# First stage: the output gate's modulation computed as rows, with waits for zeros and for a square root at other places

## The reference, cut to what matters

```
mod_lat = silu(c) @ mod_w + mod_b          # one row of 3072 for the tokens
mod_c   = silu(c_ctx) @ mod_w + mod_b      # one row of 3072 for the context
sh, sc, gt = split(mod, 3)                 # shift, scale, output gate (1024 each)
p = (layer_norm(x) * (1 + sc) + sh) @ w_in # 4224 columns: pooling, RWKV, HGRN, gate
y_rwkv, o_hgrn = the two recurrent branches, both directions, over context and tokens
mix = concat(pool, y_rwkv, o_hgrn) * silu(g)
x = layer_norm(ALPHA * x + gt_l * (mix @ w_out)) * ln_g + ln_b
```

## Time and profile before

| what | value |
|---|---|
| runs, median | 1694.6 us |
| profiled execution, its own time | 1697.69 us |
| its span | 1695.9 us |
| TensorE busy in the span | 1627.6 us (96%) |
| VectorE, ScalarE, GpSimd busy | 466.8, 325.7, 19.3 us |
| mean granted TensorE clock | 0.974 of full speed |
| DMA, share of 16 engines over the span | 33%, 191.29 MB |

### The profile page before, as it was taken

How to read it: one execution, slowest core, us unless ns; L and a number is a source line. 1 busy time by engine, 2 the same in 40 slices (tenths; PEclk the granted TensorE clock), 3 DMA queues, 4 the chain that set the end, 5 groups by cost and what they waited for, 6 DMA issues and landing times.

```text
span 1695.9 us, 26099 instructions
## 1 busy us (share of the span) xinstructions
PE 1627.6 (96%) x11627; PEld 1303.0 (77%) x11627; DVE 466.8 (28%) x1053; ACT 325.7 (19%) x689; POOL 19.3 (1%) x33
## 2 busy tenths in 40 slices
PE   7999998889799899999999999999999999999998
PEld 2544587778689687777788888888778778888887
DVE  2431023565652414124232000001402423200001
ACT  1201222443432311033300000001104330000000
POOL 2000001000000000000000000000000000000000
PEclk9999969989899999999999999999999999999999
DMA  9221330000002533433243444453343324344440
GB/s 332 103 89 60 107 117 2 3 2 3 17 25 80 126 114 135 149 113 136 100 149 128 157 155 156 149 127 123 126 149 121 128 100 149 136 157 154 149 162 25
DMA packets 110879, 191.29 MB, mean 113 GB/s; under 512 B 20888, under 2 KB 27296, under 8 KB 110640
## 3 DMA queue, kind: packets, MB, share of 16 engines
q1 hardware_dynamic: 109776, 188.29, 32.1%
q0 software_dynamic: 960, 1.33, 0.2%
q10 hardware_dynamic: 32, 0.01, 0.0%
HBM read 188.57 MB, written 1.05 MB: 112 GB/s over the span
## 4 chain that ended last, share of the span: by engine, by line
PE 79%; issue 16%; DVE 2%; ACT 1%; POOL 1%; DVEq 1%; POOLq 0%; ACTq 0%
PE psum L1071 28%; PE psum L1215 13%; PE psum L1156 9%; PE psum L793 5%; PE psum L1079 4%; PE psum L718 3%; PE psum L1239 2%; PE psum L954 1%; PE psum L1142 1%; PE psum L1185 1%; PE psum L709 1%; PE psum L1098 1%; PE psum L974 1%; ACT arena L1704 1%; PE psum L877 1%
## 5 line engine op out<-in xcount | busy, mean ns | idle before, releaser
L1071 PE MATMUL psum<-arena 128*128 128x256 f32 x2208 | 480.6, 379 | 0.0
L1071 PEld LDWEIGHTS psum<-arena 128*128 128x128 f32 x2208 | 418.1, 190 | 61.0 <-issue 1.3
L1215 PE MATMUL psum<-arena 128*128 128x256 f32 x1024 | 222.2, 379 | 0.0
L1704 ACT ACTIVATE arena<-psum 128x512 f32<-128x512 f32 (+6 forms) x228 | 118.7, 526 | 521.6 <-PE psum L1071 132.6
L1215 PEld LDWEIGHTS psum<-arena 128*128 128x128 f32 x1024 | 194.0, 189 | 27.9
L1156 PE MATMUL psum<-arena 128*128 128x256 f32 x768 | 176.6, 382 | 0.0
L1156 PEld LDWEIGHTS psum<-arena 128*128 128x128 f32 x768 | 142.1, 190 | 26.3 <-issue 5.3
L1304 PE MATMUL psum<-arena 128*128 128x512 f32 (+1 forms) x368 | 139.5, 537 | 1.2 <-issue 1.1
L1304 PEld LDWEIGHTS psum<-arena 128*128 128x128 f32 x368 | 69.1, 189 | 71.5 <-issue 69.1
L793 PE MATMUL psum<-arena 64*64 64x64 f32 x3072 | 96.6, 219 | 1.1 <-issue 1.1
L793 PEld LDWEIGHTS psum<-arena 64*64 64x64 f32 x3072 | 92.6, 135 | 6.5 <-issue 4.2
(11 more groups left out here) (315 smaller groups left out, 1333.5 us busy)
## 6 DMA issues: line engine op xcount, KB each, us to landing
arena<-in_w_in SPq DMA_DIRECT2D x33, 2048.0 KB, 7.8
arena<-in_w_up SPq DMA_DIRECT2D x16, 2048.0 KB, 8.3
arena<-in_w_down SPq DMA_DIRECT2D x16, 2048.0 KB, 7.8
arena<-in_w_out SPq DMA_DIRECT2D x6, 2048.0 KB, 7.9
arena<-in_w_branch SPq DMA_DIRECT2D x6, 2048.0 KB, 8.3
arena<-in_mod_w SPq DMA_DIRECT2D x5, 2048.0 KB, 13.7
arena<-in_w_in SPq DMA_DIRECT2D x3, 1024.0 KB, 6.8
arena<-in_w_in SPq DMA_DIRECT2D x12, 256.0 KB, 4.7
```

The lines of the kernel that those rows point to most:

```text
L1071: mm = pe.matmul(b[:, i * T:(i + 1) * T], w[:, k, c:c + P], src[:, k, :], start=k == 0, stop=k == ks - 1)
L1215: mm = pe.matmul(bs[t][:, 0:T], w[:, k, t * P:(t + 1) * P], hff[:, c * KT + k, :], start=c == 0 and k == 0, stop=c == 3 and k == KT - 1)
L1704: return act.activation(dst, src, ACT.Copy, scale=scale)
```

## The change

Four edits, all in the first block:

1. `gain(i)` takes the row form of `modulation(n)`: silu is the stationary operand, 512 columns of weights stream past, eight matmuls for a chunk in place of 32. ScalarE copies the two rows into `grow` (an alias of the RWKV buffers `ru` and `rs`, not in use yet). Eight small transposes into a new bank `gtT` make columns of both halves, behind `pmix`; VectorE adds the bias once, to all sixteen numbers of a partition.
2. The bank plan of the tail changes with it: `gt0` and `gt1` are emptied by ScalarE, and `gtT` is a new group, so that `g2` and `g3` take other banks.
3. ScalarE's wait for `stats_ready` with the square root stands behind the copies of `mod0` and `mod1`, not ahead of them.
4. The waits for `zeroed` go from the start of the scores to ScalarE's write to `acc` and to VectorE's write to `lkm`.

```
-[("gt0", "D", 1)] ... [("gt1", "D", 1)] ... [("pmix0", "D", 1), ("pmix1", "D", 1)]
+[("gt0", "A", 1)] ... [("gt1", "A", 1)] ... [("pmix0", "D", 1), ("pmix1", "D", 1), ("gtT", "D", 1)]

 TensorE, gain(i):
-for n in range(4):
-    for k in range(KT):
-        mm = pe.matmul(b[:, 2 * n:2 * n + 2], w[:, k, n * P:(n + 1) * P], silu_c[:, k, :], ...)
+for k in range(KT):
+    mm = pe.matmul(b[0:2, :], silu_c[:, k, :], w[:, k, :], start=k == 0, stop=k == KT - 1)
 TensorE, behind pmix:
+b = take_bank(tl, "gtT_0")
+tl.wait_emptied(pe, "gt1_0")
+for t in range(KT):
+    mm = turn(b[:, 2 * t:2 * t + 2], grow[0:2, t * P:(t + 1) * P])
+mm.then_inc(tl.filled, 1)

 ScalarE, setup:
-act.wait_ge(sem("stats_ready"), 1)
-act.activation(rstd4.unsqueeze(2), mv[:, :, 1:2], ACT.Sqrt, bias=eps(LN_EPS))
-done("std_ready")
 for n in range(4):
+    if n == 2:
+        act.wait_ge(sem("stats_ready"), 1)
+        act.activation(rstd4.unsqueeze(2), mv[:, :, 1:2], ACT.Sqrt, bias=eps(LN_EPS))
+        done("std_ready")
     setup.wait_filled(act, f"mod{n}")
     emptied(setup, copy(mrow[0:2, 512 * n:512 * n + 512], bank(setup, f"mod{n}")[0:2, :]))
 ScalarE, tail:
+def gain(i):
+    tl.wait_filled(act, f"gt{i}_0")
+    emptied(tl, copy(grow[0:2, 512 * i:512 * i + 512], bank(tl, f"gt{i}_0")[0:2, :]))
...
 ScalarE, start of the scores, moved to the write to acc:
-if j == 0:
-    act.wait_ge(sem("zeroed"), 1)
...
 VectorE, tail: both gain(i) go; behind pmix:
+r = slice(2 * KT, 3 * KT)
+tl.wait_filled(dve, "gtT_0")
+emptied(tl, dve.tensor_tensor(modc[:, r], bank(tl, "gtT_0")[:, 0:2 * KT]..., mb[:, r]..., ALU.add))
 VectorE, ahead of L2027, moved to the start of full_vector:
-if j == 0:
-    dve.wait_ge(sem("zeroed"), 1)
```

More of the change, by code:

```diff
@@ L460, in build @@
         vt = take(512, (4, P))
-        rh, ru, rs = take(2 * P, (2, P)), take(4 * P, (2, 2, P)), take(4 * P, (2, 2, P))
+        rh, rurs = take(2 * P, (2, P)), take(8 * P)
+        ru, rs = [rurs[:, n * 4 * P:(n + 1) * 4 * P].rearrange("p (d c t) -> p d c t", d=2, c=2) for n in range(2)]
         acc = take(8 * P, (2, 4, P))
@@ L466, in build @@
         end_first = top[0]
+        grow = rurs
         slots = [ring[:, n].rearrange("p k n -> p (k n)") for n in range(SLOTS)]
@@ L1333, in gain @@
                         b = take_bank(tl, f"gt{i}_0")
-                        for n in range(4):
-                            for k in range(KT):
-                                mm = pe.matmul(b[:, 2 * n:2 * n + 2], w[:, k, n * P:(n + 1) * P], silu_c[:, k, :], start=k == 0, stop=k == KT - 1)
+                        for k in range(KT):
+                            mm = pe.matmul(b[0:2, :], silu_c[:, k, :], w[:, k, :], start=k == 0, stop=k == KT - 1)
                         mm.then_inc(tl.filled, 1)
@@ L1690, in hgrn_scalar @@
             hg.wait_emptied(act, f"lev5_{j}")
+            if j == 0:
+                act.wait_ge(sem("zeroed"), 1)
             for r in HALVES:
@@ L1767, in tail_scalar @@
                         yield
+                    def gain(i):
+                        tl.wait_filled(act, f"gt{i}_0")
+                        emptied(tl, copy(grow[0:2, 512 * i:512 * i + 512], bank(tl, f"gt{i}_0")[0:2, :]))
                     yield
+                    gain(0)
                     yield
@@ L1773, in tail_scalar @@
                     yield
+                    gain(1)
                     yield
@@ L1909, in tail_vector @@
             def tail_vector():
[L1911 to L1915, removed]
                 for _ in range(12):
@@ L1921, in tail_vector @@
                     emptied(tl, dve.tensor_copy(pv[:, m, :], bank(tl, f"pv{m}_0")[:, 0:T]))
[L1922 to L1929, removed]
+                for _ in range(6):
+                    yield
                 for n in range(2):
@@ L1933, in tail_vector @@
                                                          mix[:, n, :], ALU.mult, ALU.mult))
+                r = slice(2 * KT, 3 * KT)
+                tl.wait_filled(dve, "gtT_0")
+                emptied(tl, dve.tensor_tensor(modc[:, r], bank(tl, "gtT_0")[:, 0:2 * KT].rearrange("p (a b) -> p a b", b=2),
+                                              mb[:, r].unsqueeze(2).to_broadcast([P, KT, 2]), ALU.add))
                 yield
@@ L2042, in full_vector @@
         def full_vector(dve, j, done, emptied, bc, fence):
+            if j == 0:
+                dve.wait_ge(sem("zeroed"), 1)
             for g, dst, masks in (("lk", lkm, ("before", "after")), ("akb", akb.rearrange("p d h m t -> p d (h m) t"), ("upto", "from"))):
```

## The result

Against the kernel before on the same chip the changed kernel took 1680.62 us (median of four, 1676.93 to 1681.52), the kernel before 1694.33 us. The ratio is 0.9913 with a 95% interval of 0.9891 to 0.9935, which is 14.7 us faster, from 11 to 18.5. A second measurement, with the other experiments, gave 1679.87 us and 0.9906 (0.9891 to 0.9921), 15.9 us.

The account below looks back on a forecast made before the run. TensorE was taken as the bound, busy nearly throughout the first stage, partly at half clock. Terms 2.2 + 13.2 - 0.5 - 0.55 + 3.3 = 17.7 us, off the 1694.6 median, gave 1676.9 us; range 1671 to 1685.

Parts of the forecast that it names:

- root: start of `mod2`: Setup: with two copies ahead of the root, `mod2` starts at 27.65 us and not 29.85, 2.2 us; ends 0 and 4.2.
- `gain(0)`: Tail, first gain: row form at full clock takes 7.13 us from start to start, not 10.01; 2.9 us less.
- `itok` and pooling: Tail, between the gains: 3.86 us at clock 0.50 before, half of it at full clock; 1.9 us less.
- `gain(1)`: Tail, second gain: 14.07 us before, 7.13 plus 0.26 of issue after; 6.7 us less.
- `diag` and `gate(0)`, less the wait ahead of `lev0`: Tail: 9.45 us before, 7.8 at full clock, 1.7 less; 0.5 given back as VectorE empties `diag` late (ends 0 and 2).
- transposes of `gtT`: Tail: eight small transposes added on the path cost half of what sixteen took, 0.55 us given back.
- scores: Start of the scores: without the wait for `zeroed`, `up` starts 3.3 us sooner; ends 0 and 4.4.
- lead at `up`: First score matmuls: all terms summed, 2.2 + 13.2 - 0.5 - 0.55 + 3.3 = 17.7 us; the rest moves as a whole.
- R1: Tail: the clock falls in the row form too, so only 5.4 us gained, 1689.2 us; chance 0.08.
- R2: Tail: ScalarE and VectorE become the bound; `diag` and `lev0` give back 4 to 5 us more, 1681 to 1682; chance 0.13.
- R3: Setup and scores: clock kept at both closed pauses too, 2.0 + 1.1 us more, 1673.8 us; chance 0.12.
- R4: Recurrences lose the clock, each microsecond costing half; 45 us more at half clock gives 1699.4 us, slower; chance 0.02.

Follow-up runs that it names:

- the run with 64 moving columns: Kernel before, only each block of weights in the gains meets 64 moving columns (silu's two, repeated 32 times), not two; 1681.77 us, ratio 0.9922.
- the first four experiments: Against the kernel before: output gate as rows only 1686.26 us; root moved only 1693.67; waits for zeros moved only 1690.97; column form with 64 moving columns 1681.77.
- the fillers at the right place: Kernel before with root and zero waits moved and 64 moving columns, plus seven idle matmuls ahead of VectorE's wait in two recurrence pauses; 1679.53 us, 1677.26 without.
- the run with both fillers and 64 columns: Kernel before with root and zero waits moved, 64 moving columns, and idle matmuls in the setup and ahead of the wait in the recurrences; 1676.44 us, ratio 0.9892.

## Why the prediction was right, and where it was off

**Point by point**, in the profiled executions:

| step | forecast, us | profile after against before, us |
|---|---|---|
| root: start of `mod2` | 2.2 | 2.1 |
| root: start of `gain(0)` | 2.2 | 207.12 - 204.83 = 2.3 |
| `gain(0)` | 2.9 | 10.01 - 7.13 = 2.9 |
| `itok` and pooling | 1.9 | 3.86 - 2.10 = 1.8 |
| `gain(1)` | 6.7 | 14.07 - 7.29 = 6.8 |
| `diag` and `gate(0)`, less the wait ahead of `lev0` | 1.7 - 0.5 | 9.45 - 8.23 = 1.2, wait 0.43 |
| transposes of `gtT` | -0.55 | -0.66 |
| scores | 3.3 | 3.8 |
| lead at `up` | 17.7 | 280.85 - 262.83 = 18.0 |

The mechanism was right in every step of the tail, and the run with 64 moving columns shows it: the clock was the whole gain of the rows. R1 is out; its ground, that either form uses two of 128 columns of the array, holds for the row form alone, since in the column form the stationary operand is 128x128. R2's wait ahead of `lev0` was 0.43 us and no more, and ahead of `diag` there was none.

**What was luck** is the second row of the table. R3 happened in part: `mod2` took 7.03 us and gave 2.0 us that the forecast put at nothing, and the scores gave 0.5. The lead was 4.1 us at `mod3`; 1.5 of it went over the first projections, and 0.3 in a longer wait for the chunk of `gain(0)` (0.82 us, 0.47 before). What was left, 2.3 us, happens to meet the forecast's 2.2. Nor does this row show the root at all: the runs with rows alone and with 64 columns alone leave it where it was and start `gain(0)` at 204.53 and 204.68 us, as early as the changed kernel. Several profiles together say more. In the six with the root moved and no filler in the setup the first 512-column projection starts at 69.95 us in the mean (68.57 to 71.51), in the five with the root in its old place at 72.03 (69.90 to 74.17). That is 2.1 us, near the forecast's term, in a scatter as large.

**The clock behind the closed pauses.** It was 1.00 over `mod2` behind sixteen transposes and a pause of 2.06 us, and 1.00 over 259.5 to 263.0 us, of which twenty transposes are the main part. But `mod2` can go either way behind the same rows. Of the nine profiles with the root moved it took 7.03 us in six, behind pauses of 1.83 to 2.85 us, and 8.48 to 8.73 in three, behind pauses of 2.47 to 2.85. The Trainium skill, "TensorE: Matmul & The Clock Gate", "Part 4: PE-mode transpose", says that transposes don't count as busy for the clock in the way that matmuls do. What the prediction made of it, that neither place would hold its clock, did not come about in the changed kernel. Whether transposes count at all is not shown, since no run here changes them alone.

**What was off** is the step from the sum to the time. I wrote that the rest of the program moves as a whole, and took the sum, made against the profiled execution, off the median.
- In the setup the 4.1 us of lead at `mod3` shrank to 2.6 at the first 512-column projection (69.78 against 72.36), since the clock was at half for 6.8 us there and for 3.4 before. In the second profiles it was 3.4 us in the changed kernel and 6.8 in the kernel before, so this too is scatter. The root alone measured 1.4 us and not 2.2, but its interval goes from 3.6 us faster to 0.7 slower.
- Behind the scores the lead went from 18.0 to 14.4 us at the start of the second block, with 17.1 + 17.1 us at half clock in the recurrences where the first profile had 13.7 + 13.7; at the end it was 16.2. In the second profiles of both kernels it was 21.8 at `up` and 21.0 at the end. So the larger part of this is scatter of single executions and no loss that the change makes.
- The profiled executions of the kernel before (1697.7 and 1701 us) are above its median of 1694 to 1695, those of the changed kernel (1681.5 and 1679.9) are within 1 us of its own. The granted clocks say the same: 0.974 and 0.971 in the profiles, 0.975 in the mean of the 23 executions that the first four experiments share. Terms read from such a profile may hold more half clock than the median has. For the rows this isn't seen: from `gain(0)` to `gate(1)` it takes 38.0 to 38.1 us in all four profiles with the old form and 25.4 in those of the rows alone and of the changed kernel. Of the three parts, the rows measured 10.7 us (7.5 to 13.9) where their terms make 13.2 - 0.5 - 0.55 = 12.2.

By the medians the rows' term was 1.5 us too large and the root's 0.8, and the zeros' 0.9 too small; each of the three still lies within its interval, as 17.7 does within those of both measurements of the whole, so that the miss of 3 us is hardly beyond what these runs can tell. Why profiled executions of the kernel before fall above its median was not found. The record shows only this much: in all four profiles of kernels whose tail is at half clock (the kernel before twice, the root alone, the waits for zeros alone) the profiled execution is the longest of its kernel, while that of the rows alone is the shortest of six.

The range was added up wrongly as well: the terms' own ends make 2.2 + 1.5 + 3.3 = 7.0 us to the slow side (3.6 to the fast side), and the prediction says at most 4 to either. At 7.0 the range would have ended at 1684 us, so the stated end of 1685 covers it all the same.

R4, a loss in the recurrences, is not seen beyond this scatter: from `up` to the end it takes 1.3 us more in the changed kernel's two profiles than in those of the kernel before. Half clock there is mostly hidden behind VectorE and ScalarE: the fillers at the right place took 10.2 us of it out of the first recurrence and won 0.8 us at most. So R4's price of half a microsecond for each was too high.

## What to carry to other kernels

When a stretch of full TensorE runs at half clock, look at how many columns stream past each weight load. With two columns the clock fell here, and the dense work behind them ran at half clock too; repeating the columns 32 times (7.36 us for a chunk, 7.03 in the row form) gave the same gain as a new form with rows, transposes and copies. A filler (matmuls whose result nobody reads) gained 1.1 us in the profiles where TensorE's own work stands behind the pause, as in the setup, and nothing clear where another engine bounds it; and it must stand ahead of the wait that makes the pause. One profile can't tell a term of 2 us from scatter where the clock comes and goes: lay several side by side. Take a sum made from one profile to a median only after asking whether that execution's granted clock is that of the others.

## What the runs showed of the hardware

- 64 records of 128x64 matmuls took 7.36 us at clock 1.00, 115 ns each. The column form with two columns ran 39 records in 4.4 us, 113 ns each, at clock 0.99. So here 62 more float32 columns cost 2 ns for each record.
- The spread of one kernel's executions follows its granted clock: the 23 executions of the kernel before that the first four experiments share go from 1687.27 us at 0.979 to 1702.82 us at 0.971.
- The same pause of 2.85 us behind sixteen transposes left the clock at 1.00 over `mod2` in one execution (7.03 us, the run with both fillers and 64 columns), and was followed by half clock for part of it in another (8.73 us, the run with the fillers in the recurrences).
- In the kernel before, the clock fell while TensorE was busy for 4.38 of 4.40 us, and in its second profile it fell twice in the same way, with 128x2 matmuls each time.
